# Attention in unbroken runs of turns, scores and values, with the PSUM banks dealt out anew and the scores moved to SBUF by VectorE

## The chip, the cores and the metric

The kernel runs on one core of one Trainium2 chip. The metric is the device time of the whole program in microseconds, as the median of the runs. Everything below is about three stages of a long program; the rest of the program is the same before and after.

## The reference, cut to what matters

The program is two small diffusion-transformer blocks of two layers each, on 512 latent tokens and 256 context tokens of width 1024, all in fp32. Three of its four mixers are attention:

```
def diff_attend(q, k, v, lam):                      # layer 1: 8 heads x 2 maps, 768 keys
    s = jnp.einsum('bqhmd,bkhmd->bhmqk', q, k).astype(jnp.float32) * ATTN_SCALE
    p = jax.nn.softmax(s, axis=-1)
    w = (p[:, :, 0] - lam * p[:, :, 1]).astype(v.dtype)
    return jnp.einsum('bhqk,bkhe->bqhe', w, v)
# layer 2, neighbourhood: 16 heads, a bias on the 512 latent keys, 256 context keys without one
        s_loc = jnp.where(col_in[None, None, :, None, :], s_loc + bias[None].astype(jnp.float32), -jnp.inf)
        s_all = jnp.concatenate([s_loc.reshape(B, NA_HEADS, GRID_W, n_loc), s_ctx], axis=-1)
        prob = jax.nn.softmax(s_all, axis=-1).astype(v_band.dtype)
# layer 3, window: 16 heads, keys at most 128 away and the context, and one sink logit per head
        s_win = jnp.where(ok, s_win, NEG_INF)
        p = sink_softmax(jnp.concatenate([s_win, s_ctx], axis=-1)).astype(vw.dtype)
```

## The kernel before, in words

`attention_stage` is called three times, with `diff=True` (the differential stage), `bias=True` (the bias stage) and `sink=True` (the sink stage). Its work is cut into units. A unit is one pair of heads (or of maps), m = 0 and 1, and one tile of 128 queries; its keys come in blocks of 128, nk of them. There are 8 pairs. In the differential stage a pair has six units in the order 6, 2, 6, 2, 6, 6 key blocks (48 units: I call those with six large, those with two small). In the bias stage a pair has four units of six blocks (32 units). In the sink stage a pair has six units of 4, 2, 5, 2, 5, 4 blocks (48 units).

Each unit goes through these steps, on queues written out by hand. Each engine has its own loop over s, and semaphores tie them:

- TensorE computes scores. The head m uses rows 64m to 64m+63 of the array, so that the two heads of a pair can run side by side. One fp32 matmul is two passes in the trace, and so two records.
- VectorE finds each row's minimum of the (negated) scores (`minima`); in the bias stage it first adds the bias `G`.
- ScalarE makes the exponentials and their sums (`probabilities`).
- VectorE inverts the sums (`inverse_sums`), and in the differential stage combines the two maps into one weight (`combine`).
- TensorE turns the weights, 128 by 128 at a time, four in one PSUM bank (a chunk). It uses the whole array. There are one or two chunks for a unit of the differential stage, three in the bias stage, one to three in the sink stage.
- ScalarE and, for chunk 1 outside the differential stage, VectorE copy the turned blocks to SBUF (`pT_mat`).
- TensorE multiplies them with the values (`weighted`), and VectorE scales the result (`finish`). Outside the differential stage the two heads of `weighted` use different columns of the array.

PSUM has eight banks. Before, the scores of one unit take three banks, columns of m = 0 from the left and of m = 1 from the right, and units take turns on two such sets (banks 0 to 2 and 3 to 5). Banks 6 and 7 (`TB`) take the turned chunks by turns, and bank 7 also the result of `weighted`, and bank 6 the side work on the modulation matrix (`mod_rows`, one per pair, in the differential stage). A score set is free again when ScalarE has read it (`p_done` of the unit two before). Because a set of banks is shared between chunks, results and heads, TensorE's loop deals the work out in pieces:

```
                if s >= 0:
                    turn(s, 0)
                if s + ahead < N:
                    scores_early(s + ahead)
                if s >= 0 and len(chunks[s]) > 1:
                    turn(s, 1)
                if s + ahead < N:
                    scores_late(s + ahead)
                if s >= 0 and len(chunks[s]) > 2:
                    turn(s, 2)
```

and then the modulation and `weighted(s - 1)`. `ahead` is 3 in the differential stage and 2 elsewhere: so far the scores run ahead of the turns.

## Time and profile before

| what | value |
|---|---|
| median of 3 runs | 3873.28 us (3869.57 to 3876.15) |
| span of the profiled execution | 3870.4 us |
| TensorE busy / VectorE busy / ScalarE busy in it | 95% / 57% / 35% |
| differential stage | from 256.0 us, some 208 us |
| bias stage | from 1301.0 us, some 179 us |
| sink stage | from 2035.6 us, some 202 us |
| mean granted TensorE clock | 0.985 |

The times are of the device, of the one core. The span is that of one execution under the profiler, from its first to its last instruction; it stands 2.9 us below the median of the timed runs. PE is TensorE's matmul queue, PEld its weight loads, DVE VectorE, ACT ScalarE, POOL GpSimd. In a timeline each row is a group of like instructions: start in us, duration in us from the first start to the last end, engine, line of the kernel, operation, tiles, how many, and in brackets how long the engine had stood idle and what ended that. `issue` there means that nothing the profile shows released it.

### The profile page before, as it was taken

To read this page: it belongs to the slowest core of one execution; us is meant where nothing else is said; L and a number is where in the kernel's file an instruction comes from. 1 tells how busy PE (TensorE), PEld (TensorE's weight loads), DVE (VectorE), ACT (ScalarE), POOL (GpSimd) and SP (SyncE) were. 2 spreads that over 40 slices of the span, in tenths; PEclk is the share of its full clock that TensorE was granted. 3 is DMA by queue.
4 is the path that set the end of the run, shared out by engine and by line. 5 is a ranking of instruction groups with operands and counts; after the bars stand their busy time and mean duration, and the time that the engine had idled before them with its cause. 6 is when DMAs were issued, how large, how long until landed. Compare 5 with 4: busy or idle time off the path is not lost. (4 is left out here: it accounts for less than half of the span.)

```text
span 3870.4 us, 54090 instructions
## 1 busy us (share of the span) xinstructions
PE 3668.5 (95%) x20171; PEld 2984.9 (77%) x20171; DVE 2209.8 (57%) x3167; ACT 1338.7 (35%) x2342; POOL 833.0 (22%) x588
## 2 busy tenths in 40 slices
PE   7988899999999899999999999999989998899998
PEld 5876688888878677777786678888878876687886
DVE  5746646556573475444436647656665637846445
ACT  3346532121243454222325522212123334523222
POOL 2500012313132111222220011221310007901222
PEclk9999999999999999999999999999999999999999
DMA  5134223322322311544320013233221141032222
GB/s 183 66 120 131 66 77 115 114 100 102 113 67 68 85 45 42 188 152 155 113 65 10 1 44 135 104 113 114 105 74 55 57 142 33 23 109 96 98 93 72
DMA packets 191993, 352.38 MB, mean 91 GB/s; under 512 B 42236, under 2 KB 43853, under 8 KB 191821
## 3 DMA queue, kind: packets, MB, share of 16 engines
q1 hardware_dynamic: 187693, 340.83, 26.4%
q10 hardware_dynamic: 4144, 9.44, 0.7%
q8 instruction: 102, 1.67, 0.2%
q14 instruction: 54, 0.44, 0.0%
HBM read 341.71 MB, written 16.92 MB: 93 GB/s over the span
## 5 line engine op out<-in xcount | busy, mean ns | idle before, releaser
L569 POOL TENSOR_TENSOR x<-x,scaled_buf 128x512 f32<-128x512 f32 (+1 forms) x360 | 495.1, 1391 | 2202.1 <-DVE scaled_buf L561 2201.7
L129 DVE TENSOR_TENSOR w_lo<-raw,w_hi 128x2048 fp32r<-128x2048 f32 x198 | 465.6, 2351 | 685.0 <-ACT w_hi L123 675.7
L123 ACT ACTIVATE w_hi<-raw 128x2048 fp32r<-128x2048 f32 x197 | 377.1, 1914 | 1286.3 <-PE psum L386 1283.9
L384 PE MATMUL psum<-hT_hi,w_hi 128*128 128x512 f32 (+1 forms) x1888 | 669.0, 354 | 2.4 <-DVE hT_lo L848 1.5
L385 PE MATMUL psum<-hT_lo,w_hi 128*128 128x512 f32 (+1 forms) x1888 | 665.1, 352 | 0.0
L386 PE MATMUL psum<-hT_hi,w_lo 128*128 128x512 f32 (+1 forms) x1888 | 664.5, 352 | 0.0
L384 PE MATMUL psum<-w_hi,uT_hi 128*128 128x512 f32 x1280 | 503.0, 393 | 0.0
L386 PE MATMUL psum<-w_hi,uT_lo 128*128 128x512 f32 x1280 | 498.7, 390 | 0.0
L385 PE MATMUL psum<-w_lo,uT_hi 128*128 128x512 f32 x1280 | 498.2, 389 | 0.0
L561 DVE TENSOR_TENSOR scaled_buf<-psum,gate 128x512 f32<-128x512 f32 x360 | 244.8, 688 | 337.3 <-PE psum L386 291.9
L384 PE MATMUL psum<-w_hi,hT_hi 128*128 128x512 f32 x1072 | 419.8, 392 | 2.2 <-issue 1.2
L386 PE MATMUL psum<-w_hi,hT_lo 128*128 128x512 f32 x1072 | 417.6, 390 | 0.0
L385 PE MATMUL psum<-w_lo,hT_hi 128*128 128x512 f32 x1072 | 417.3, 389 | 0.0
L384 PEld LDWEIGHTS psum<-hT_hi,w_hi 128*128 128x128 f32 x1888 | 358.4, 190 | 51.4 <-DVE hT_lo L848 1.9
L385 PEld LDWEIGHTS psum<-hT_lo,w_hi 128*128 128x128 f32 x1888 | 358.4, 190 | 48.0
L386 PEld LDWEIGHTS psum<-hT_hi,w_lo 128*128 128x128 f32 x1888 | 357.8, 190 | 48.7
L384 PEld LDWEIGHTS psum<-w_hi,uT_hi 128*128 128x128 f32 x1280 | 240.4, 188 | 51.1 <-issue 3.5
L386 PEld LDWEIGHTS psum<-w_hi,uT_lo 128*128 128x128 f32 x1280 | 240.3, 188 | 50.8
L385 PEld LDWEIGHTS psum<-w_lo,uT_hi 128*128 128x128 f32 x1280 | 240.6, 188 | 48.0
L384 PEld LDWEIGHTS psum<-w_hi,hT_hi 128*128 128x128 f32 x1072 | 201.6, 188 | 44.8 <-issue 3.6
L386 PEld LDWEIGHTS psum<-w_hi,hT_lo 128*128 128x128 f32 x1072 | 201.4, 188 | 42.1
L385 PEld LDWEIGHTS psum<-w_lo,hT_hi 128*128 128x128 f32 x1072 | 201.6, 188 | 40.9
(286 smaller groups left out, 4918.4 us busy)
## 6 DMA issues: line engine op xcount, KB each, us to landing
raw<-in_w_mlp SPq DMA_DIRECT2D x64, 1024.0 KB, 5.2
raw<-in_ff_w SPq DMA_DIRECT2D x64, 1024.0 KB, 5.3
mod_wide<-in_w_mod SPq DMA_DIRECT2D x32, 1536.0 KB, 8.5
mod_wide<-in_w_mod SPq DMA_DIRECT2D x8, 3072.0 KB, 10.5
raw<-in_ssm_w_in SPq DMA_DIRECT2D x20, 1024.0 KB, 5.1
mod_slab<-in_w_mod SPq DMA_DIRECT2D x8, 2048.0 KB, 8.4
raw<-in_a_w_qkv SPq DMA_DIRECT2D x12, 1024.0 KB, 5.1
raw<-in_b_w_qkv SPq DMA_DIRECT2D x12, 1024.0 KB, 5.1
```

Source lines behind the costliest of these rows:

```text
L123: act.activation(K.w_hi[h][:, :, :], K.raw[h][:, :, :], ACT.Copy).then_inc(K.hi_done.h, 1)
L129: dve.tensor_tensor(K.w_lo[h][:, :, :], K.raw[h][:, :, :], K.w_hi[h][:, :, :].bitcast(F32), ALU.subtract).then_inc(K.lo_done.h, 1)
L384: pe.matmul(out, hi_a, hi_w, start=first, stop=False, **check)
L385: pe.matmul(out, hi_a, lo_w, start=False, stop=False, **check)
L386: return pe.matmul(out, lo_a, hi_w, start=False, stop=last, **check)
L561: dve.tensor_tensor(K.scaled_buf[:, j % 2, :], bank[:, :], K.gate[:, cls, ds(n * SLAB_N, SLAB_N)], ALU.mult)\
L569: pool.tensor_tensor(x, x, K.scaled_buf[:, j % 2, :], ALU.add).then_inc(K.added.h, 1)
```

## The change

What it does:

- The scores of head m have two banks of their own (0 and 1, 2 and 3), and there is one such set instead of two. The turned chunks 0, 1 and 2 have a bank each (4, 5 and 6; 4 and 5 in the differential stage). The result of `weighted` has its own bank (7; 6 in the differential stage, where the modulation has 7).
- TensorE's loop becomes: all turns of unit s, all scores of unit s + ahead, [modulation,] all of `weighted(s - 1)`. `ahead` is 4 and 3. A unit's score matmuls are up to 512 keys wide, and alternate between the heads.
- VectorE no longer only reads the scores to find the minimum: `taken` copies them from PSUM to `p_mat` in SBUF, with the minimum as the second output; in the bias stage the addition of the bias writes there too. ScalarE's exponential then works in place in SBUF.
- The next unit's scores wait for that copy (`s_read`, one count per head) where they waited for ScalarE two units back.
- VectorE's order is changed: inverse (and combine) first, then the copy of chunk 1 (as before, outside the differential stage), minima, finish. ScalarE copies its chunks together.
- `p_mat` has four slots in the differential stage, three elsewhere.

The diff, cut to what the text speaks of:

```
-        self.nk = len(keys[0])
-        self.width = self.nk * P
-        self.at = (0, 12 - self.nk)
-        self.shares = self.nk > 4
+        self.nk = len(keys)
+        self.at = (0, self.nk)
...
+        runs = []
+        for i, kt in enumerate(self.keys):
+            if runs and i % 4 and self.keys[i - 1] == kt - 1 and (kt in self.unrotated) == (kt - 1 in self.unrotated):
+                runs[-1][2] += 1
+            else:
+                runs.append([i, kt, 1])
+        return runs
...
-    ahead = 3 if diff else 2
+    ahead = 4 if diff else 3
+    p_mat, pT_mat = (K.p_mat_diff, K.pT_mat_diff) if diff else (K.p_mat, K.pT_mat)
...
-    scores_of = [K.psum[:, 3 * b:3 * b + 3, :].rearrange("p a b -> p (a b)") for b in range(2)]
-    S = lambda v: scores_of[v % 2]
-    TB = [K.bank[6], K.bank[7]]
-    ap0, sharing = K.apart.n, [sum(u.shares for u in units[:v]) for v in range(N + 1)]
+    S = [K.psum[:, 2 * m:2 * m + 2, :].rearrange("p a b -> p (a b)") for m in range(2)]
+    TB = [K.bank[4 + c] for c in range(2 if diff else 3)]
+    OB, MB = (K.bank[6], K.bank[7]) if diff else (K.bank[7], None)
...
-            def turn(v, c):
-                b = c % 2
-                if c == 0 and diff:
+            def turns(v):
+                if diff:
                     pe.wait_ge(K.w_done.h, at(K.w_done, v))
-                elif c == 0:
+                else:
                     pe.wait_ge(K.p_done.h, at(K.p_done, 2 * v + 1))
-                pe.wait_ge(K.pt_read[b].h, at(K.pt_read[b], order[v, c] - 1))
-                if b == 1:
-
-                    pe.wait_ge(K.o_read.h, at(K.o_read, v - 2))
-                for i, col in enumerate(chunks[v][c]):
-                    mm = pe.transpose(TB[b][:, i * P:(i + 1) * P], K.p_mat[:, v % 3, col * P:(col + 1) * P], K.ident[:, :])
-                mm.then_inc(K.pt_done[b].h, 1)
-
-            def score(v, run, opens):
+                for c, blocks in enumerate(chunks[v]):
+                    pe.wait_ge(K.pt_read[c].h, at(K.pt_read[c], order[v, c] - 1))
+                    for i, col in enumerate(blocks):
+                        mm = pe.transpose(TB[c][:, i * P:(i + 1) * P], p_mat[:, v % ahead, col * P:(col + 1) * P], K.ident[:, :])
+                    mm.then_inc(K.pt_done[c].h, 1)
+
+            def scores(v):
                 u = units[v]
-                _, m, col, kt, n = run
-                rows = slice(m * HEAD_DIM, (m + 1) * HEAD_DIM)
-                return pe.matmul(S(v)[:, col * P:(col + n) * P], q_of(u.pair, u.tile, kt in u.unrotated)[rows, :],
-                                 k_of(u.pair, kt, n, rows), start=opens, stop=True, skip_group_check=True)
-
-            def scores_early(v):
-                u = units[v]
-
-                pe.wait_ge(K.p_done.h, at(K.p_done, 2 * (v - 2) + 1))
-                for run in u.segments()[0]:
-                    mm = score(v, run, True)
-                    if u.shares and run[1] == 1:
-                        mm.then_inc(K.apart.h, 1)
-                if not u.segments()[1]:
-                    mm.then_inc(K.s_done.h, 1)
-
-            def scores_late(v):
-                u = units[v]
-                opened = set(run[2] // 4 for run in u.segments()[0])
-                for m in range(2):
-                    for kt, mask in u.masks.items():
-                        col = u.at[m] + u.keys[m].index(kt)
-                        pe.matmul(S(v)[:, col * P:(col + 1) * P], K.ident_a[:, :], mask, start=col // 4 not in opened, stop=True,
+                opened = set()
+                for kt, mask in u.masks.items():
+                    for m in range(2):
+                        col = u.keys.index(kt)
+                        if not opened or opened == {(0, col // 4)}:
+                            pe.wait_ge(K.s_read.h, at(K.s_read, 2 * (v - 1) + m))
+                        pe.matmul(S[m][:, col * P:(col + 1) * P], K.ident_a[:, :], mask, start=(m, col // 4) not in opened, stop=True,
                                   skip_group_check=True)
-                        opened.add(col // 4)
-                for run in u.segments()[1]:
-                    if u.shares and run[2] // 4 == 1:
-
-                        pe.wait_ge(K.apart.h, ap0 + sharing[v] + 1)
-                    mm = score(v, run, run[2] // 4 not in opened)
-                    opened.add(run[2] // 4)
-                if u.segments()[1]:
-                    mm.then_inc(K.s_done.h, 1)
+                        opened.add((m, col // 4))
+                for col, kt, n in u.segments():
+                    for m in range(2):
+                        rows = slice(m * HEAD_DIM, (m + 1) * HEAD_DIM)
+                        if col == 0 and not u.masks:
+                            pe.wait_ge(K.s_read.h, at(K.s_read, 2 * (v - 1) + m))
+                        mm = pe.matmul(S[m][:, col * P:(col + n) * P], q_of(u.pair, u.tile, kt in u.unrotated)[rows, :],
+                                       k_of(u.pair, kt, n, rows), start=(m, col // 4) not in opened, stop=True, skip_group_check=True)
+                        opened.add((m, col // 4))
+                mm.then_inc(K.s_done.h, 1)
...
                 if s >= 0:
-                    turn(s, 0)
+                    turns(s)
                 if s + ahead < N:
-                    scores_early(s + ahead)
-                if s >= 0 and len(chunks[s]) > 1:
-                    turn(s, 1)
-                if s + ahead < N:
-                    scores_late(s + ahead)
-                if s >= 0 and len(chunks[s]) > 2:
-                    turn(s, 2)
+                    scores(s + ahead)
                 if s in rows_at:
-                    modulation_rows(s)
-                if s in cols_at:
-                    modulation_columns(s)
+                    modulation_rows(rows_at[s])
                 if s >= 1:
                     weighted(s - 1)
+                if s in cols_at:
+                    modulation_columns(cols_at[s])
             weighted(N - 1)
...
-            def copied(v, c):
-                dst, src = turned(act, v, c)
-                act.activation(dst, src, ACT.Copy).then_inc(K.pt_read[c % 2].h, 1)
+            def copied(v):
+                act.wait_ge(K.o_done.h, at(K.o_done, v - 2))
+                for c, blocks in enumerate(chunks[v]):
+                    if c == 1 and not diff:
+                        continue
+                    act.wait_ge(K.pt_done[c].h, at(K.pt_done[c], order[v, c]))
+                    n = len(blocks) * P
+                    act.activation(pT_mat[:, v % 2, c * 4 * P:c * 4 * P + n], TB[c][:, 0:n], ACT.Copy).then_inc(K.pt_read[c].h, 1)
...
                 for m in range(2):
-                    act.activation(K.p_mat[:, v % 3, u.span(m)], S(v)[:, u.span(m)], ACT.Exp, bias=K.neg_max[:, v % 4, m:m + 1],
+                    if diff:
+                        act.wait_ge(K.s_read.h, at(K.s_read, 2 * v + m))
+                    p = p_mat[:, v % ahead, u.span(m)]
+                    act.activation(p, p, ACT.Exp, bias=K.neg_max[:, v % 4, m:m + 1],
                                    scale=-1.0, accum_out=K.p_sum[:, v % 4, m:m + 1]).then_inc(K.p_done.h, 1)
...
+                if v >= ahead:
+                    for c in range(len(chunks[v - ahead])):
+                        dve.wait_ge(K.pt_done[c].h, at(K.pt_done[c], order[v - ahead, c]))
+                nm, p = K.neg_max[:, v % 4, :], p_mat[:, v % ahead, :]
+                taken = lambda m, a, b, low: dve.tensor_scalar(p[:, (u.at[m] + a) * P:(u.at[m] + b) * P], S[m][:, a * P:b * P], 1.0, 3e38,
+                                                               ALU.mult, ALU.min, accum_out=low)
                 if bias:
                     if u.tile == 0:
                         dve.wait_ge(K.g_ready.h, at(K.g_ready, u.pair))
                     row = N_ROWS - 1 - 2 * u.tile
                     for m in range(2):
-                        x = s[:, 0:4 * P] if m == 0 else s[:, 8 * P:12 * P]
                         g = K.G[u.pair % 2][:, m, row:row + N_ROWS, :].rearrange("p r c -> p (r c)")
-                        dve.tensor_tensor_reduce(x, x, g, 1.0, 3e38, ALU.add, ALU.min, nm[:, m:m + 1])
-                    link(dve.tensor_reduce(K.ctx_min[:, v % 4, :], s[:, 4 * P:8 * P].rearrange("p (m c) -> p m c", m=2), AX.X, ALU.min))
+                        dve.tensor_tensor_reduce(p[:, u.at[m] * P:(u.at[m] + LAT_TILES) * P], S[m][:, 0:N_LAT], g, 1.0, 3e38, ALU.add, ALU.min,
+                                                 nm[:, m:m + 1])
+                        taken(m, LAT_TILES, TOK_TILES, K.ctx_min[:, v % 4, m:m + 1]).then_inc(K.s_read.h, 1)
+                    dve.wait_ge(K.s_read.h, at(K.s_read, 2 * v + 1))
                     dve.tensor_tensor(nm, nm, K.ctx_min[:, v % 4, :], ALU.min).then_inc(K.nm_done.h, 1)
                     return
-                if u.nk == 6:
-                    ins = dve.tensor_reduce(nm, s.rearrange("p (m c) -> p m c", m=2), AX.X, ALU.min)
-                else:
-                    for m in range(2):
-                        ins = dve.tensor_reduce(nm[:, m:m + 1], s[:, u.span(m)], AX.X, ALU.min)
...
             for s in range(-ahead, N):
-                if diff and 0 <= s + 1 < N:
-                    combine(s + 1)
+                if 0 <= s + ahead - 2 < N:
+                    inverse_sums(s + ahead - 2)
+                    if diff:
+                        combine(s + ahead - 2)
                 if not diff and s >= 0 and len(chunks[s]) > 1:
-                    dst, src = turned(dve, s, 1)
-                    dve.tensor_copy(dst, src).then_inc(K.pt_read[1].h, 1)
+                    copied(s, 1)
...```

How the change moves TensorE's instructions in the steady part of the bias stage. A row is one line's matmuls in program order; `p_mat` is turned, `qkv` gives queries and keys, `pT_mat` is multiplied with the values, `p_inv` spreads the inverse sums. Before, one unit:

```order
L1722 MATMUL psum<-ident,p_mat 128x128 x4
L1729 MATMUL psum<-qkv 128x256 x2
L1722 MATMUL psum<-ident,p_mat 128x128 x4
L1729 MATMUL psum<-qkv 128x256
L1729 MATMUL psum<-qkv 128x512
L1729 MATMUL psum<-qkv 128x256
L1722 MATMUL psum<-ident,p_mat 128x128 x4
L1778 MATMUL psum<-pT_mat,qkv 64x128 x12
L1783 MATMUL psum<-ident,p_inv 64x128 x2
```

And after the change, one unit:

```order
L1703 MATMUL psum<-ident,p_mat 128x128 x12
L1722 MATMUL psum<-qkv 128x512 x2
L1722 MATMUL psum<-qkv 128x256 x2
L1740 MATMUL psum<-pT_mat,qkv 64x128 x12
L1745 MATMUL psum<-ident,p_inv 64x128 x2
```

Three groups of turns and two of scores have become one group each; the number of turned blocks and of key columns is the same.

VectorE in the same place of the bias stage, one unit before the change. L1887 is the addition of the bias with its minimum (and, in the row after it, the read-out of the minimum):

```order
L1939 COPY pT_mat<-psum 128x512
L1887 ISA psum,neg_max<-psum,G_128 128x512
L1887 ISA neg_max 128x1
L1887 ISA psum,neg_max<-psum,G_128 128x512
L1887 ISA neg_max 128x1
L1888 TENSOR_REDUCE ctx_min<-psum 128x2
L1889 TENSOR_TENSOR neg_max<-neg_max,ctx_min 128x2
L1909 RECIPROCAL p_inv<-p_sum 128x2
L1928 COPY inv_rows<-psum 128x128
L1929 TENSOR_TENSOR qkv<-psum,inv_rows 128x128
```

And after it:

```order
L1873 COPY pT_mat<-psum 128x512
L1838 ISA p_mat,neg_max<-psum,G_130 128x512
L1838 ISA neg_max 128x1
L1830 TENSOR_SCALAR p_mat,ctx_min<-psum 128x256
L1838 ISA p_mat,neg_max<-psum,G_130 128x512
L1838 ISA neg_max 128x1
L1830 TENSOR_SCALAR p_mat,ctx_min<-psum 128x256
L1842 TENSOR_TENSOR neg_max<-neg_max,ctx_min 128x2
L1881 COPY inv_rows<-psum 128x128
L1882 TENSOR_TENSOR qkv<-psum,inv_rows 128x128
L1859 RECIPROCAL p_inv<-p_sum 128x2
```

One reduction over both heads' context columns has become two copies with a minimum, and the reciprocal has moved behind the finish.

VectorE in the differential stage, one large unit's minimum among its neighbours, before (L1892 is the minimum of both maps in one instruction):

```order
L1892 TENSOR_REDUCE neg_max<-psum 128x2
L1909 RECIPROCAL p_inv<-p_sum 128x2
L1913 TENSOR_SCALAR p_inv<-p_sum,p_inv,neg_lam 128x1
L1926 TENSOR_SCALAR qkv<-psum,p_inv 128x128
L1919 SCALAR_TENSOR_TENSOR p_mat<-p_mat,p_inv 128x256
```

And after:

```order
L1830 TENSOR_SCALAR p_mat_diff,neg_max<-psum 128x768 x2
L1879 TENSOR_SCALAR qkv<-psum,p_inv 128x128
L1859 RECIPROCAL p_inv<-p_sum 128x2
L1865 TENSOR_SCALAR p_inv<-p_sum,p_inv,neg_lam 128x1
L1867 SCALAR_TENSOR_TENSOR p_mat_diff<-p_mat_diff,p_inv 128x256
```

One instruction over 1536 columns has become two over 768, and inverse and combination of a unit now stand together, after the finish.

## Rows read from the trace of the kernel before

**Rows 1.** The stages: window, its us, busy PE, PEld, DVE, ACT, POOL, PEclk, DMA.

```profile
256.00:464.00 208.00, 174.60 (x1216) 120.85 (x1216) 139.58 (x272) 128.59 (x378) 0.00 (x0) 0.98 0.42 122
1301.00:1480.30 179.30, 168.51 (x1600) 122.91 (x1600) 117.98 (x320) 96.27 (x193) 27.24 (x6) 0.97 0.15 36
2035.60:2237.60 202.00, 183.54 (x1728) 131.44 (x1728) 130.37 (x417) 101.36 (x305) 0.00 (x0) 0.97 0.01 1
```

**Rows 2.** Timeline, bias stage, one unit's step in the steady part.

```profile
1400.95 0.42 PEld L1722 LDWEIGHTS psum<-ident,p_mat 128*128 128x128 f32 x4 [0.17 <-issue]
1401.54 0.30 PEld L1729 LDWEIGHTS psum<-qkv 64*128 64x128 f32 x4 [0.17 <-issue]
1402.17 0.42 PEld L1722 LDWEIGHTS psum<-ident,p_mat 128*128 128x128 f32 x4 [0.33 <-issue]
1402.75 0.73 PEld L1729 LDWEIGHTS psum<-qkv 64*128 64x128 f32 x6 [0.17 <-issue]
1403.81 0.42 PEld L1722 LDWEIGHTS psum<-ident,p_mat 128*128 128x128 f32 x4 [0.33 <-issue]
1403.94 0.70 DVE L1887 CUSTOM_DVE_ANT_0 psum<-psum,G 128x512 f32<-128x512 f32 x1 [0.38 <-PE psum L1729]
1404.40 1.29 PEld L1778 LDWEIGHTS psum<-pT_mat,qkv 128*64 128x64 f32 x24 [0.17 <-issue]
1404.55 0.73 DVE L1887 CUSTOM_DVE_ANT_0 psum<-psum,G 128x512 f32<-128x512 f32 x1
1405.20 0.69 DVE L1888 TENSOR_REDUCE ctx_min<-psum 128x2 f32<-128x512 f32 x1
1406.08 0.42 PEld L1722 LDWEIGHTS psum<-ident,p_mat 128*128 128x128 f32 x4 [0.17 <-issue]
```

**Rows 3.** Timeline, bias stage, behind its last scores: eight turns in a row.

```profile
1469.72 1.12 PE L1722 MATMUL psum<-ident,p_mat 128*128 128x128 f32 x8 [0.22 <-DVE qkv L1929]
```

**Rows 4.** Timeline, sink stage: one row a pair apart, and a small unit's values.

```profile
2080.29 0.16 DVE L1899 TENSOR_TENSOR neg_max<-neg_max,sink_neg 128x2 f32<-128x2 f32 x1
...
2104.26 0.16 DVE L1899 TENSOR_TENSOR neg_max<-neg_max,sink_neg 128x2 f32<-128x2 f32 x1
...
2110.41 0.42 PEld L1778 LDWEIGHTS psum<-pT_mat,qkv 128*64 128x64 f32 x8 [0.17 <-issue]
...
2111.21 0.42 PEld L1722 LDWEIGHTS psum<-ident,p_mat 128*128 128x128 f32 x4 [0.17 <-issue]
```

**Rows 5.** Timeline, differential stage: modulation rows a pair apart, and values.

```profile
394.94 1.90 PE L942 MATMUL psum<-mod_slab,cT 128*2 128x512 f32 x16
396.77 1.60 PE L1776 MATMUL psum<-qkv,pT_mat 128*128 128x128 f32 x12
...
420.04 1.90 PE L942 MATMUL psum<-mod_slab,cT 128*2 128x512 f32 x16
```

**Rows 6.** Groups of instructions by line and shape, VectorE: busy us, mean ns.

```profile
L1892 DVE TENSOR_REDUCE neg_max<-psum 128x2 f32<-128x1536 f32 x32 | 56.2, 1755 | 22.0 <-PE psum L1729 21.8
L1895 DVE TENSOR_REDUCE neg_max<-psum 128x1 f32<-128x256 f32 x64 | 24.0, 416 | 0.5
L1634 DVE TENSOR_SCALAR qkv<-psum 128x512 f32<-128x512 f32 x28 | 18.1, 686 | 34.1 <-PE psum L1616 34.1
L1887 DVE DVE_READ_ACCUMULATOR2_ANT neg_max<- 128x1 f32 x64 | 9.1, 142 | 0.0
L1919 DVE SCALAR_TENSOR_TENSOR p_mat<-p_mat,p_inv 128x768 f32<-128x768 f32 x32 | 32.3, 1010 | 0.1
L1939 DVE COPY pT_mat<-psum 128x512 f32<-128x512 f32 x64 | 44.3, 692 | 70.0 <-PE psum L1722 70.0
```

**Rows 7.** Groups of instructions by line and shape, ScalarE: from PSUM, from SBUF.

```profile
L1827 ACT ACTIVATE pT_mat<-psum 128x256 f32<-128x256 f32 x64 | 24.6, 384 | 30.4 <-PE psum L1722 30.4
L1827 ACT ACTIVATE pT_mat<-psum 128x512 f32<-128x512 f32 x144 | 86.0, 597 | 194.5 <-PE psum L1722 194.5
L1981 ACT ACTIVATE hT_hi<-qkv 128x1024 fp32r<-128x1024 f32 x10 | 9.7, 1046 | 10.7 <-PEq L1685 10.7
```

More of the change, by code:

```diff
@@ L1521, in segments @@
     def segments(self):
[L1525 to L1537 removed]
+        runs = []
[5 more added lines that the diff above has]
+        return runs
     def chunks(self, heads):
[L1541 removed]
+        blocks = range(heads * self.nk)
         return [blocks[c:c + 4] for c in range(0, len(blocks), 4)]
@@ L1829, in probabilities @@
             def probabilities(v):
                 u = units[v]
-                act.wait_ge(K.nm_done.h, at(K.nm_done, v))
-                if v >= 3:
-                    for b in range(2):
-                        if last_turn(v - 3, b) is not None:
-                            act.wait_ge(K.pt_done[b].h, at(K.pt_done[b], last_turn(v - 3, b)))
+                if bias or sink:
+                    act.wait_ge(K.nm_done.h, at(K.nm_done, v))
                 if sink:
@@ L3210, in program @@
         mixed = [0, 4, 1, 5, 2, 3]
-        attention_stage(K, [Unit(p, t, (every if t < LAT_TILES else [4, 5],) * 2) for p in range(PAIRS) for t in mixed], q_of, k_of,
+        attention_stage(K, [Unit(p, t, every if t < LAT_TILES else [4, 5]) for p in range(PAIRS) for t in mixed], q_of, k_of,
                         lambda pair, m, kt: K.qkv[:, kt, 2 * D + pair * P:2 * D + (pair + 1) * P],
```

161 lines of the change are left out of this document (68 added, 93 removed).

## The prediction, made before the changed kernel was run

> **What bounds the kernel now.** I read the clock and the share of each engine first, then the three attention stages as windows [rows 1], then the waits and the timeline inside each. Only these stages change. TensorE is busy for 175 of 208 us, 169 of 179 and 184 of 202; VectorE for 140, 118 and 130; DMA is idle or nearly so in two of them. So TensorE sets the pace, and what is to be read is how its time is spent. The bias stage shows it best, since it repeats exactly [rows 2]: a step takes 1406.08 - 1400.95 = 5.13 us, and consists of turns 0.59, early scores 0.63, turns 0.58, late scores 1.06, turns 0.59, values 1.68. Nothing outside TensorE is waited for. But each time that its use of the array changes (whole for turns, rows in halves for scores, columns in halves for values) the weight loads stand idle for 0.17 us, and 0.33 us behind scores, released by nothing. The early group has 256 columns for each head, the late one 512, and the difference is 0.43 us: so a score group costs 0.20 us plus 0.43 for each two key blocks of both heads. A pass over 128 columns costs 0.11 us when it stands in a run (12 passes to the next load: (1.60 - 0.27)/12, [rows 5]; eight turns last 1.12 with the tail of 0.27, [rows 3]).
>
> The other two stages repeat by pairs: 2104.26 - 2080.29 = 23.97 us in the sink stage [rows 4], 420.04 - 394.94 = 25.10 us in the differential stage [rows 5]. Of the latter TensorE is busy 84%: there it also waits for the engines around it.
>
> **The change, part by part.**
>
> Bias stage, TensorE. Twelve turns in a run: 0.59 + 8 x 0.11 = 1.47. One score group: 0.63 + 2 x 0.43 = 1.49. Values as before, 1.68. The step becomes 4.64 us, 0.49 less. No column is saved; what goes is two turn groups' and one score group's change of array use. 30 full steps give 15 us.
>
> Is TensorE then still the bound? VectorE is busy 118.0/32 = 3.69 us per unit [rows 1]. It loses the context minimum (0.69, [rows 2]) and gains two copies of 256 columns with a minimum. The trace shows no such operation. Its floor is the plain reduction of as many columns, 0.416, without a read-out; my price adds the read-out of 0.142 [rows 6]. That the copy itself is not dearer is seen at 512 columns, where a tensor_scalar from PSUM takes 0.686, as long as the minimum over the context. So + 2 x 0.56 - 0.69 = + 0.43, and 4.1 us of 4.64: TensorE remains the bound.
>
> The new wait: the scores of unit v + 1 wait for VectorE's copy of unit v, since there is one score set. Behind that wait stand the next values and turns on TensorE. Scores that start at 0 are seen by VectorE at 1.49 + 0.13 (1403.94 is 1.19 behind 1402.75, for a group of 1.06). It then takes 0.65 + 0.42 for each head and 0.14 for the last read-out: released at 3.9 us. TensorE wants them at 4.64. The wait is covered, by values and turns, with 0.7 us to spare; without that cover each 0.1 us costs 3 us in the stage.
>
> Sink stage, per pair (22 key blocks in six units). TensorE: 44 turns x 0.11 and 0.15 for each of six groups, 5.7; scores 22 x 0.215 + 6 x 0.20 = 5.9; twelve masks at 0.11, 1.3; values: the two-block unit takes 2111.21 - 2110.41 = 0.80 [rows 4], six blocks 1.68 [rows 2], so 0.22 a block and 0.36 a unit, 7.0. Sum 19.9. VectorE: 130.4/8 = 16.3 [rows 1], and twelve read-outs, 18.0. The units differ in size, and a step of TensorE joins the turns of one, the scores of another and the values of a third: taking step by step whichever engine is later I get 20.3, and allow 0.4 for late releases: 20.7 against 23.97, 8 x 3.3 = 26 us.
>
> Differential stage, per pair. TensorE: 28 turns 3.7, scores 4 x 1.49 + 2 x 0.63 = 7.2, values 56 passes x 0.11 = 6.2, modulation 1.83 (396.77 - 394.94) and its turns 0.4, changes of use 0.5: 19.8. VectorE: 139.6/8 = 17.5 [rows 1]. Two copies of 768 columns cost 2 x (0.95 + 0.14) = 2.2 for one reduction of 1.755: the 0.95 is the line through 256 and 512 columns, (0.686 - 0.416)/256 = 1.05 ns a column [rows 6]. Four times + 0.43 and twice + 0.28: 19.7. The two sums are equal, but not the steps. In the order of the six steps TensorE needs 3.2, 5.5, 1.5, 4.1, 1.9, 3.7 from one unit's scores to the next (the 5.5: modulation rows 1.83, values 1.33, turns 0.86, scores 1.49), VectorE 3.1, 3.7, 3.7, 3.0, 3.1, 2.6 (minima, finish, inverse, and 1.01 us of combination for a large unit, [rows 6]). With one score set neither can be more than a fraction of a unit ahead, about 1.5 us behind the release for a large one. Walked through, the steps are 3.5, 5.5, 3.7, 3.1, 3.1, 3.3: 22.2 against 25.1, 8 x 2.8 = 22 us after rounding down. So here the modulation rows, squeezed between scores and values, keep a part of the gain.
>
> ScalarE. Its exponentials now read SBUF. From PSUM 256 columns take 384 ns and 512 take 597, by which 1024 would take 1023; from SBUF they take 1046 [rows 7]. So 23 ns for each of 256 exponentials, 6 us of an engine that is busy for 129 of 208 us where it is fullest, and idle for TensorE's turns: nothing. The Trainium skill, VectorE: DVE Perf Modes, section on the TRN2 errata, gives ScalarE 224 cycles of fixed cost from SBUF and 172 from PSUM, an estimate of 43 ns each and 11 us in all. The trace shows about half of that; the sum would be the same by either.
>
> Ends of the stages. One more unit is scored before the first turn, each one behind VectorE's copy: some 2 to 3 us more per stage. At the other end the last steps have no scores: in the bias stage two such units now take 1480.3 - 1469.7 = 10.6 us; afterwards three follow at 1.47 + 1.68 = 3.15 each. I take these as even. The lower bound has them as a gain of 6 us in the bias stage.
>
> Sum: 15 + 26 + 22 = 63 us. 3870.4 - 63 = 3807 for the profiled execution, whose span lies 2.9 us below the median: **3810 us**.
>
> **The rivals.**
>
> 1. The forecast: TensorE's rhythm shortens in all stages and few waits replace what went. 3788 to 3832. For it: rows 2, where every idle stretch of the loads is a change of use. 0.55.
>
> 2. Better still: no release is late. Differential 19.9 (- 42), sink 19.9 (- 32), bias with its end (- 21): 3778. Against it stand the unequal steps. 0.08.
>
> 3. The single score set becomes the bound: VectorE's copy comes later than counted (semaphores, a copy that waits for the turns), 0.3 us in each of 128 units. 63 - 38 = 25 us: 3848. For it: in the differential stage both engines are at 19.7 of 22. 0.22.
>
> 4. Given back in full, or a stage held by something else (the modulation's loads): 3873. Against it: DMA works 42% of the stage's time. 0.05.
>
> 5. Slower: the copy with a minimum runs at a lower rate than the reduction. If it takes twice as long, VectorE needs 19.7 + 9.3 = 29.0 a pair in the differential stage (+ 31 us), 23.9 in the sink stage (none), 5.0 in the bias stage (- 5): 3899. It decides from about 1.8 times the price, 1.7 us for 768 columns. For it: a combination of two inputs takes 1010 ns for 768 columns, and the operation is new here. Against it: the bias addition with its minimum costs 0.61 to 0.65 per 512 columns [rows 2], hardly more than a reduction. 0.10.
>
> **How the numbers follow.** A measurement of this kernel can tell about 0.2%, 7.7 us, from no change. Rivals 1 to 3 are faster: 0.85; same 0.05; slower 0.10. The range holds the first case, most of the third and a part of the second: 3785 to 3858; the likeliest case's own is 3788 to 3832.
>
> **What would show it.** Bias stage: a step of 4.6 us, with one idle 0.33 us and two of 0.17 before loads. Sink: 20 to 21.5 us a pair. Differential: 22 to 23.5, TensorE waiting for VectorE after small units and VectorE for TensorE after the modulation rows. The copy of 768 columns at 0.95 us. Wrong would be: a copy over 1.3 us, scores that wait for `s_read` in every step, turns that wait for the combination, or a bias step over 4.9.

## The result

The changed kernel takes 3803.09 us (3802.08 to 3803.63, four runs) against 3874.55 us before (3869.57 to 3876.15, four runs). The ratio is 0.9815, with a 95% interval of 0.9801 to 0.9829: 71.5 us or 1.85% faster. 3810 was predicted, with 3785 to 3858. The profiled execution has a span of 3800.3 us against 3870.4, 70.1 us less.

The three stages, as windows from the first scores to the last `finish` (us, busy PE, PEld, DVE, ACT, POOL, then the granted clock, DMA share and GB/s), to be held against [rows 1]:

```profile
255.90:441.30 185.40, 176.74 (x1152) 118.81 (x1152) 146.96 (x400) 127.76 (x376) 0.00 (x0) 0.99 0.48 137
1279.60:1442.50 162.90, 155.07 (x1536) 114.99 (x1536) 120.47 (x416) 98.87 (x193) 27.30 (x6) 0.97 0.17 40
1998.30:2167.00 168.70, 164.73 (x1728) 134.08 (x1728) 128.95 (x513) 104.75 (x305) 0.00 (x0) 0.98 0.01 2
```

| stage | before | after | less | predicted |
|---|---|---|---|---|
| differential | 207.6 | 185.4 | 22.2 | 22 |
| bias | 179.2 | 162.8 | 16.4 | 15 |
| sink | 201.6 | 168.7 | 32.9 | 26 |

The columns before and after are the first scores' start to the last `finish`, from the two traces. They add up to 71.5, against 70.1 between the spans of the same two traces: the three stages hold the whole gain. Ahead of, between and behind them no stretch changed by more than 1.0 us, and together these are 1.4 us longer. TensorE is busy for 95% of the differential stage, where it was busy for 84% before; its work hardly changed (174.6 to 176.7 us), but its pauses went.

The steady step of the bias stage, in the timeline (start, us, engine, line, operation, tiles, and in brackets the idle time before it and what ended it); it answers to [rows 2]:

```profile
1358.26 1.29 PEld L1703 LDWEIGHTS psum<-ident,p_mat 128*128 128x128 f32 x12 [0.17 <-issue]
1359.72 0.30 PEld L1722 LDWEIGHTS psum<-qkv 64*128 64x128 f32 x4 [0.17 <-issue]
...
1361.21 1.29 PEld L1740 LDWEIGHTS psum<-pT_mat,qkv 128*64 128x64 f32 x24 [0.33 <-issue]
1361.33 0.69 DVE L1838 CUSTOM_DVE_ANT_0 p_mat<-psum,G 128x512 f32<-128x512 f32 x1 [1.25 <-PE psum L1722]
...
1362.89 1.19 PEld L1703 LDWEIGHTS psum<-ident,p_mat 128*128 128x128 f32 x11 [0.17 <-issue]
1363.25 0.08 DVE L1830 DVE_READ_ACCUMULATOR p_mat<-psum 128x1 f32 x1
```

Twelve turns take 1.46, the one score group 1.49, the values 1.68: 4.63 us, where the prediction had 1.47, 1.49, 1.68 and 4.64. Of the six idle stretches that a step had for a change of array use, three are left: 0.17, 0.17 and 0.33. VectorE has read the second head 3.61 us after the scores started (1363.33 - 1359.72; predicted 3.9), 1 us before TensorE wants the bank (1364.35).

The sink stage repeats after exactly 20.0 us, where [rows 4] had 23.97, and the differential stage after 22.09, where [rows 5] had 25.10:

```profile
2042.70 0.16 DVE L1849 TENSOR_TENSOR neg_max<-neg_max,sink_neg 128x2 f32<-128x2 f32 x1
...
2062.70 0.16 DVE L1849 TENSOR_TENSOR neg_max<-neg_max,sink_neg 128x2 f32<-128x2 f32 x1
```

```profile
338.79 1.90 PE L942 MATMUL psum<-mod_slab,cT 128*2 128x512 f32 x16
...
360.88 1.90 PE L942 MATMUL psum<-mod_slab,cT 128*2 128x512 f32 x16
```

The new operations, in the groups by line and shape (busy us, mean ns, idle before them), beside [rows 6, 7]:

```profile
L1830 DVE TENSOR_SCALAR_CACHE_REDUCE p_mat_diff<-psum 128x768 f32<-128x768 f32 x64 | 58.8, 955 | 11.2 <-PE psum L1722 11.2
L1830 DVE TENSOR_SCALAR_CACHE_REDUCE p_mat<-psum 128x256 f32<-128x256 f32 x96 | 39.1, 419 | 1.8 <-PE psum L1722 1.8
L1830 DVE DVE_READ_ACCUMULATOR p_mat<-psum 128x1 f32 x160 | 13.2, 83 | 0.0
L1792 ACT ACTIVATE p_mat<-p_mat,neg_max 128x768 f32<-128x768 f32 x64 | 59.0, 925 | 11.2 <-DVE neg_max L1842 11.2
```

The copy with a minimum costs what the bare minimum of as many columns costs (0.955 us for 768 columns, as the bare minimum in experiment 4; 0.419 for 256, where the bare minimum had 0.416), and its read-out takes 83 ns. The prediction had priced it by the 142 ns of the bias addition's read-out in the kernel before. The exponential of 768 columns takes 925 ns from SBUF against 898 from PSUM.

In the waits of the differential stage (us in total, times, longest, from 280 to 410 us) rival 3 can be seen, in small:

```profile
PEld psum L1738 <- issue: 14.8, 35, 0.9
...
DVE qkv L1879 <- PE psum L1738: 10.8, 12, 1.5
PEld psum L1722 <- DVE p_mat_diff L1830: 9.3, 23, 0.6
...
DVE p_mat_diff L1830 <- PE psum L1722: 5.5, 23, 0.3
```

The score loads wait for VectorE's copy 23 times, for 9.3 us in six pairs (some of them hold the 0.17 us that a change of use costs anyway), and VectorE waits for TensorE elsewhere: each in turn, as the prediction's walk through the steps had it.

The prediction did not look at the clock at the start of a stage. In the last 10 us ahead of the changed kernel's bias stage TensorE is busy for 1.8 us, and the granted clock is 0.81; in the first 15 us of the stage it is 0.67, as in the kernel before. In three of the experiments it is 0.50 there, which is the lower of the two levels (1.2 and 2.4 GHz) all the time; why it differs from one execution to another is open. Stages with the same code differ by some 2 us along with it (experiment 5), so a difference of that size can't be put down to an edit without a look at the pairs.

### The profile page after: what moved, and what is told of

The parts are those of the page before. It is cut to its first block and busy times, and to the rows that moved or that the text cites. A ratio compares the mean times of both kernels' runs of the same rounds, so it can differ in the third digit from the quotient of the medians.

```text
span 3800.3 us, 53965 instructions
## 1 busy us (share of the span) xinstructions
PE 3639.9 (96%) x20043; PEld 2979.6 (78%) x20043; DVE 2219.4 (58%) x3487; ACT 1344.4 (35%) x2342; POOL 831.7 (22%) x588
```

## The experiments

Each was timed beside the kernel before, on the same chip; the ratios are to that kernel. "Changed kernel" is the one whose result stands above. It was not timed again beside the experiments, where the kernel before took 3875.3 to 3878.0 us, so differences to 3803 us are good to some 4 us. Pair and step lengths are repeats of the same instruction in the trace.

**1. Pieces again** (`e1_split`). The banks, the copies and VectorE's order stay as in the changed kernel, but TensorE deals its work out in pieces again. The first two key blocks of each head's scores also get a matmul of their own again (not shown), which makes two more score matmuls in a unit of six key blocks; the late score group still takes the 1.06 us that it took before.

```diff
                 if s >= 0:
-                    turns(s)
+                    turns(s, 0)
                 if s + ahead < N:
-                    scores(s + ahead)
+                    scores(s + ahead, False)
+                if s >= 0:
+                    turns(s, 1)
+                if s + ahead < N:
+                    scores(s + ahead, True)
+                if s >= 0:
+                    turns(s, 2)
```

> The changed kernel, with TensorE's loop dealt out in pieces again: turns of chunk 0, scores of the first two key blocks, turns of chunk 1, the other scores, turns of chunk 2. Banks, the copy by VectorE, and how far the scores run ahead stay as changed. Theory 1 (the gain is the changes of array use that went): the bias step returns from 4.63 to 5.13 us, the sink pair from 20.0 to about 22, the differential pair from 22.2 to about 23: 15 + 16 + 6 = 37 us more than the changed kernel's 3803, so 3840. Theory 2 (the gain is in waits: private banks, scores further ahead): less than 10 us more, 3803 to 3813.

Measured: 3850.09 us (3848.07 to 3857.53), ratio 0.9937 (0.9918 to 0.9955). That is 47 us above the changed kernel. The differential pair is 23.34 us long, the sink pair 21.97, the bias step about 5.2. So two thirds of the gain hang on the runs themselves, with all else in place, which is theory 1. By stage, from first scores to last `finish`, the pieces give back 17.1 us in the bias stage, which is all that it had gained, 19.6 of 32.9 in the sink stage and 11.3 of 22.2 in the differential stage. The rest in these two came with the other parts of the change (a bank for each chunk, the copy, VectorE's new order, scores further ahead), and no run divides it among them.

The time is 10 us above theory 1. Eight times the change of a pair gives 39 of the 48 us by which the three stages are longer in the traces; the rest lies mostly at their starts. From the bias stage's first scores to its first `finish` it is 28.3 us here and 21.5 in the changed kernel. The first 15 us of that stage, here and in the changed kernel:

```profile
1291.30:1306.30 15.00, 12.59 (x42) 7.94 (x42) 6.35 (x27) 5.77 (x10) 0.00 (x0) 0.50 0.00 0
...
1279.60:1294.60 15.00, 12.67 (x42) 6.74 (x44) 7.22 (x30) 6.79 (x12) 0.00 (x0) 0.67 0.00 0
```

The clock was granted at 0.50 here and at 0.67 there. How much of the 6.8 us is the clock and how much the pieces was not measured.

**2. No copy** (`e2_nocopy`). VectorE only reduces, and ScalarE's exponential reads the scores from PSUM, so that the one score set is free only when ScalarE is done.

```diff
-pe.wait_ge(K.s_read.h, at(K.s_read, 2 * (v - 1) + m))
+pe.wait_ge(K.p_done.h, at(K.p_done, 2 * (v - 1) + m))
...
-                    act.activation(p, p, ACT.Exp, bias=K.neg_max[:, v % 4, m:m + 1],
+                    act.activation(p, S[m][:, 0:u.nk * P], ACT.Exp, bias=K.neg_max[:, v % 4, m:m + 1],
```

> The changed kernel without the move of the scores to SBUF: VectorE only finds the minimum (and adds the bias in PSUM), ScalarE reads the scores from PSUM, and the next scores wait for ScalarE's exponentials of the unit before, as they must with one score set. Theory 1 (the copy is what makes one score set enough): a bias step becomes turns 1.5, ScalarE's copies and exponentials to 4.5, scores to 6.0, values 1.7: 7.7 us for 4.63, + 89 us; differential about 33 a pair, + 90; sink + 70; together about 4050 (3990 to 4110). Theory 2 (the copy is no necessity, ScalarE lets go of the scores early enough): at most + 30, 3833.

Measured: 4161.16 us (4149.98 to 4169.16), ratio 1.0741 (1.0719 to 1.0763). The waits of this kernel from 340 to 420 us, and the window:

```profile
PEld psum L1722 <- ACT p_mat_diff L1792: 26.0, 24, 2.2
PE psum L1722 <- ACT p_mat_diff L1792: 19.3, 16, 2.0
```

```profile
340.00:420.00 80.00, 61.92 (x300) 39.60 (x299) 37.62 (x77) 30.86 (x96) 0.00 (x0) 0.83 0.27 79
```

The scores now wait for ScalarE, and a differential pair takes 37 to 41 us. Runs of turns with one score set are worth nothing without the copy; the copy that frees the set is the part that everything else leans on. Theory 1 is right in kind, but the time lies outside its range, 110 us above its number. The clock has a part in that: in this stretch TensorE is busy 77% of the time and the granted clock is 0.83, where the changed kernel has 98% and 1.00 in the same stretch. So the work between the waits ran slower too. How the 110 us divide between waits and clock was not measured.

**3. One unit less ahead** (`e3_shallow`), with the buffers as many as before.

```diff
-    ahead = 4 if diff else 3
+    ahead, slots = (3, 4) if diff else (2, 3)
```

> The changed kernel with the scores one unit less ahead of the turns (3 in the differential stage, 2 in the others), all slots kept. Theory 1 (depth only covers; what pays is runs): bias stage the same, since the exponentials end some 2.9 us behind the turns before and the next turns come 3.2 us behind them; differential the same; sink about + 3 us a pair, since there scores and values together can last less than the exponentials; 3 x 2.5 us less at the starts: about 3818 (3800 to 3835). Theory 2 (depth is what pays): + 50 us or more, 3853 and up.

Measured: 3803.14 us (3802.22 to 3806.67), ratio 0.9810 (0.9794 to 0.9826): the same as the changed kernel. But that is a sum of two signs. The differential pair falls from 22.09 to 21.52 us and the stage is 4.9 us shorter; the sink pair rises from 20.00 to 20.95 and the stage is 7.8 us longer. The depth pays in the sink stage and costs in the differential one; why it costs there was not tried. The prediction gave the depth neither a gain nor a loss but the ends of the stages.

**4. VectorE reads everything twice** (`e4_twice`). A second minimum of the same columns, whose result nobody uses, stands ahead of each copy.

```diff
+                        dve.tensor_reduce(K.sink_exp[:, v % 4, m:m + 1], S[m][:, LAT_TILES * P:TOK_TILES * P], AX.X, ALU.min)
...
+                    dve.tensor_reduce(K.ctx_min[:, v % 4, m:m + 1], S[m][:, 0:u.nk * P], AX.X, ALU.min)
```

> The changed kernel, and ahead of each copy of scores VectorE reads the same columns once more for a minimum that nobody uses (in the bias stage the context columns alone). That is what the copy would cost at twice its price (rival 5 of the prediction). By the prediction's arithmetic: VectorE becomes the bound in the differential stage (about 27.8 us a pair for 22.2, + 45) and in the sink stage (about 24 for 20.0, + 31), and nothing happens in the bias stage (0.7 us for each unit within a slack of about 1 us): 3803 + 76 = 3879. If VectorE's work were covered everywhere, as its busy share of 58% suggests: less than + 10.

Measured: 3922.37 us (3922.28 to 3923.61), ratio 1.0120 (1.0103 to 1.0136). The extra work on a large unit, and the differential stage from 340 to 420 us, its waits and its window:

```profile
L1846 DVE TENSOR_REDUCE ctx_min<-psum 128x1 f32<-128x768 f32 x64 | 61.1, 955 | 16.6 <-PE psum L1722 16.3
```

```profile
PEld psum L1722 <- DVE p_mat_diff L1830: 18.5, 16, 1.4
PE psum L1722 <- DVE p_mat_diff L1830: 12.1, 16, 1.1
```

```profile
340.00:420.00 80.00, 67.88 (x371) 43.65 (x371) 68.66 (x155) 40.90 (x120) 0.00 (x0) 0.87 0.38 112
```

The differential pair takes 29 to 33 us, the sink pair 24.42, the bias step 4.92. So VectorE's time between scores and release is what decides between gain and loss. Against the changed kernel 119 us were lost, not 76: 72 in the differential stage where 45 were expected, 41 in the sink stage for 31, and 8 in the bias stage for nothing. In the differential stage neither engine is full (TensorE 85%, VectorE 86%), and TensorE's loads and matmuls stand for VectorE's copy, 18.5 and 12.1 us in 16 times each. The granted clock, 0.87, is lower here too.

**5. A minimum of one input** (`e5_one_input`), in the bias stage.

```diff
-                    dve.tensor_tensor(nm, nm, K.ctx_min[:, v % 4, :], ALU.min).then_inc(K.nm_done.h, 1)
+                    dve.tensor_reduce(nm, K.ctx_min[:, v % 4, :, :], AX.X, ALU.min).then_inc(K.nm_done.h, 1)
```

The reason for it is a row of the changed kernel's trace. This instruction on two columns, 0.16 us as a rule, takes 2.2 to 3.3 us once per pair:

```profile
1360.98 4.55 POOL L1548 TENSOR_TENSOR G<-G,col_mask 128x2048 f32<-128x2048 f32 x1 [14.35 <-DMA G<-skewed_rest]
...
1363.37 2.19 DVE L1842 TENSOR_TENSOR neg_max<-neg_max,ctx_min 128x2 f32<-128x2 f32 x1
...
1366.23 0.99 PE L1740 MATMUL psum<-pT_mat,qkv 128*64 128x128 f32 x14 [0.32 <-DVE qkv L1882]
```

It ends 0.01 to 0.03 us after GpSimd's instruction, six times of six, and then `finish` and TensorE are late.

> The changed kernel, but in the bias stage the two minima of a head are written side by side and their minimum is a reduction of one input (128x4 to 128x2) and no longer a tensor_tensor of two inputs in SBUF. Nothing else changes. Theory 1: the tensor_tensor of two columns, which takes 160 ns as a rule and 2.2 to 3.3 us once in each pair in which GpSimd masks the next bias, is held by GpSimd's instruction, since both have two inputs in SBUF. Then no small operation of VectorE lasts over 0.3 us in the bias stage, its pairs take 18.5 us each (4 x 4.63) in place of 18.8 to 19.7, and the time falls by 3 to 5 us: 3799 (3796 to 3801). Theory 2: VectorE is held by GpSimd whatever the form of the instruction, or by the data of the bias: the reduction takes 2 to 3 us in its place, and the time stays at 3803 (3801 to 3806).

Measured: 3801.78 us (3797.52 to 3802.87), ratio 0.9806 (0.9793 to 0.9820). In the trace the stall is gone, in every pair:

```profile
L1842 DVE TENSOR_REDUCE neg_max<-ctx_min 128x2 f32<-128x4 f32 x32 | 5.0, 157 | 1.1
```

The pairs of the bias stage take 18.52 us each, where the changed kernel has 18.9 to 19.7, and the stage is 2.5 us shorter. So theory 1 holds for the mechanism. The time of the whole kernel misses its range (3796 to 3801), and 1.3 us can't be told from nothing. The trace says what hides the 2.5 us: the differential stage, whose code is the same and whose pairs take the same 22.09 us, is 2.1 us longer, all of it ahead of the first `finish`. The first 15 us of the differential stage, here and in the changed kernel:

```profile
255.50:270.50 15.00, 12.15 (x38) 6.27 (x38) 8.81 (x25) 8.10 (x19) 0.00 (x0) 0.68 0.74 211
...
255.90:270.90 15.00, 11.29 (x42) 5.51 (x42) 10.50 (x30) 9.21 (x21) 0.00 (x0) 0.89 0.72 211
```

The granted clock was 0.68 here and 0.89 there, and 38 matmul passes were done instead of 42.

**6. Modulation moved** (`e6_moved`), in the differential stage.

```diff
-    rows_at = {v: units[v].pair for v in range(N) if mod and units[v].tile == LAT_TILES}
-    cols_at = {v: units[v].pair for v in range(N) if mod and units[v].tile == LAT_TILES + 1}
+    rows_at = {v: units[v].pair for v in range(N) if mod and units[v].tile == 1}
+    cols_at = {v: units[v].pair for v in range(N) if mod and units[v].tile == 2}
```

> The changed kernel, but in the differential stage TensorE's modulation rows are issued in the second step of a pair and the modulation columns in the third, where it scores small units, and no longer in the fifth and sixth. Theory 1 (the prediction's walk through the steps): the 5.5 us step of the rows splits into two even ones, and what stays is the later of both engines' sums: a pair of 20.5 to 21.6 us in place of 22.15, 4 to 13 us in all, 3797 (3790 to 3800). Theory 2: the pair is held by VectorE's copies and the single score set in every step, so the place of 1.83 us of TensorE makes no difference: 3803 (3800 to 3806).

Measured: 3792.44 us (3788.62 to 3793.60), ratio 0.9780 (0.9767 to 0.9794), 10.6 us below the changed kernel. One pair later in the trace:

```profile
335.83 1.90 PE L942 MATMUL psum<-mod_slab,cT 128*2 128x512 f32 x16
356.34 1.90 PE L942 MATMUL psum<-mod_slab,cT 128*2 128x512 f32 x16
```

20.51 us a pair in place of 22.09. The prediction's long step was real: the rows of 1.83 us, squeezed between large scores and large values, kept VectorE waiting. In the changed kernel it stands still for 1.52 us a pair for the values behind the rows:

```profile
342.26 0.35 DVE L1879 TENSOR_SCALAR qkv<-psum,p_inv 128x128 f32<-128x128 f32 x1 [1.52 <-PE psum L1738]
```

With the rows moved, the longest such wait is 0.6 us.

**7. All copies on ScalarE** (`e7_scalar_copies`), in the bias and the sink stage.

```diff
-                    if c == 1 and not diff:
-                        continue
...
-                if not diff and s >= 0 and len(chunks[s]) > 1:
-                    copied(s, 1)
```

> The changed kernel, but ScalarE copies the second group of turned probabilities too in the bias and the sink stage, and VectorE none. Theory 1 (TensorE's own sums set the pace there, both engines have slack): ScalarE goes from 64 to about 78% busy, VectorE from 80 to 65%, and the time stays within 3 us of the changed kernel's: 3803 (3800 to 3808). Theory 2 (VectorE's release of the single score set is what the step waits for): the release comes up to 0.69 us earlier where the copy stood before it, and the time falls by 5 us or more, to 3798 or less. Theory 3: ScalarE, which must copy three groups and make two exponentials in a row, becomes late with the probabilities: turns wait for it, 0.2 us or more a step in 80 steps, 3819 or more.

Measured: 3803.32 us (3800.86 to 3805.88), ratio 0.9812 (0.9799 to 0.9826). The sink pair stays at 20.00 us. That VectorE copies the second group makes no difference: both engines have room for it, and TensorE's own sum sets the pace of these two stages. That is theory 1.

**8. Turns in two groups** (`e9_two_turn_groups`).

```diff
                 if s >= 0:
-                    turns(s)
+                    turns(s, False)
                 if s + ahead < N:
                     scores(s + ahead)
+                if s >= 0:
+                    turns(s, True)
```

> The changed kernel, but a unit's turns are issued in two groups, the first (four key blocks) ahead of the scores and the rest behind them; scores and values stay as they are. So each unit of more than four blocks of turns has one more group of turns and one more change of TensorE's array use, and nothing else. Theory 1 (a change of array use costs TensorE its idle of the weight loads, 0.15 us a turn group, whatever the other engines do): the bias step goes from 4.63 to 4.78 us, the sink pair from 20.0 to about 20.6 (four of six units have more than one group), the differential pair by as much or less, since it is not at TensorE's own sum; together 32 x 0.15 + 32 x 0.15 + up to 32 x 0.15, so 10 to 14 us: 3813 to 3817. Theory 2 (the gain came from the turns being early, so that copies of VectorE and ScalarE have more time, and not from the number of groups): the late turns make copies late by more than a turn group, and the time rises by over 25 us, to 3828 or more. Theory 3 (groups cost nothing by themselves): 3803.

Measured: 3827.27 us (3824.87 to 3828.17), ratio 0.9877 (0.9859 to 0.9895): 24 us, where theory 1 had 10 to 14 and theory 2 over 25. Neither number is met. The sink pair is at 21.27, the differential at 23.03, the bias pair at 19.51. The timeline of the bias stage says why:

```profile
1360.58 1.33 PEld L1724 LDWEIGHTS psum<-qkv 64*128 64x128 f32 x8 [0.17 <-issue]
...
1362.24 0.85 PEld L1705 LDWEIGHTS psum<-ident,p_mat 128*128 128x128 f32 x8 [0.33 <-issue]
1362.94 0.69 DVE L1877 COPY pT_mat<-psum 128x512 f32<-128x512 f32 x1 [1.44 <-PE psum L1705]
...
1365.45 0.08 DVE L1834 DVE_READ_ACCUMULATOR p_mat<-psum 128x1 f32 x1
1365.54 0.35 PEld L1724 LDWEIGHTS psum<-qkv 64*128 64x128 f32 x4 [0.17 <-DVE p_mat L1834]
```

VectorE stands idle for 1.44 us until the late group of turns comes, and only then turns to its minima. It ends them at 1365.53, just when TensorE wants the bank. So the second group costs twice: its own change of use, and a late release.

**9. The same, with all copies on ScalarE** (`e10_two_groups_scalar`), which takes that copy out of VectorE's way: the edits of 7 and 8 together.

> As the kernel with two turn groups, but ScalarE copies the second group of turned probabilities in the bias and the sink stage, so that VectorE no longer waits there for the turns behind the scores (1.44 us idle in a bias step of the run before) ahead of its minima. Theory 1: of the 0.32 us that a second turn group cost, 0.15 is TensorE's change of use and the rest is the second head's scores, released 0.17 us late by VectorE. Then the bias step becomes 4.78 us, the sink pair 20.6, the differential pair stays at 23.03, where ScalarE made the copies already: 162 + 5, 168 + 5, 192 us, and the time 3827 - 5 - 5 = 3817 (3814 to 3820). Theory 2: a second turn group costs 0.32 on TensorE by itself: bias step 4.95, sink pair 21.3, 3827. Theory 3: the late copy makes ScalarE late in its place (two copies and two exponentials behind the turns): 3827 or more.

Measured: 3820.22 us (3817.31 to 3820.53), ratio 0.9856 (0.9839 to 0.9872). The sink pair falls from 21.27 to 20.71, 0.71 above the changed kernel's for four units with a second group: 0.18 a group, near the 0.15 of theory 1. The bias stage kept most of its loss (steps up to 4.90, where theory 1 had 4.78), and so the time is just above theory 1's range of 3814 to 3820. There the wait only moved:

```profile
DVE p_mat L1840 <- PE psum L1705: 37.4, 22, 2.4
```

From 1320 to 1430 us VectorE's minima wait for the turns themselves, because they write into the `p_mat` slot that the late group still reads. So a price near 0.15 is shown in the sink stage alone.

**10. Three edits together** (`e8_together`): 5, 6, and in the differential stage three units ahead (four slots kept), with three ahead elsewhere.

```diff
-    ahead = 4 if diff else 3
+    ahead, slots = (3, 4) if diff else (3, 3)
```

> The changed kernel with three edits: the minimum of one input in the bias stage, the modulation rows and columns in the second and third step of a pair, and in the differential stage scores three units ahead and no longer four (the stage in which the shallower kernel was 4.9 us shorter between its first scores and its last values; the sink stage, where it was 7.9 us longer, keeps three units ahead). If the three gains add: 4 + 6 + 5 = 15 us, 3788 (3782 to 3794). If moving the rows and the shallower depth give the same slack back, 4 + 6 = 10 us: 3793. If only the first holds: 3799.

Measured: 3781.69 us (3778.15 to 3783.53), ratio 0.9754 (0.9740 to 0.9767), the fastest of all: 21.4 us below the changed kernel, where the three gains as expected added up to 15; it lies just below the expected 3782 to 3794. In the trace the differential stage is 17.2 us shorter than the changed kernel's and the bias stage 5.1. Half of the latter is the edit (2.5 in experiment 5); the other half lies ahead of the first `finish`, where the granted clock in the first 15 us was 0.78 here and 0.50 in experiment 5. The pairs take 19.97, 18.52 and 20.00 us, and from 280 to 410 us TensorE's row shows no idle time:

```profile
280.00:410.00 130.00, 130.00 (x938) 88.72 (x936) 115.96 (x330) 102.11 (x310) 0.00 (x0) 1.00 0.57 164
```

## Why the prediction was right

- **What bounds the kernel** (TensorE's rhythm, with the changes of array use as what is to be had): right, and shown by experiments 1 and 7, and by 9 for the sink stage. The Trainium skill, TensorEngine Tiling (Array Packing), Key Properties, says that changing the tiling mode drains TensorE. The rows agree: the weight loads idle for 0.17 us at each change of use, and 0.33 behind scores.
- **Bias stage, - 15**: - 16.4. The step was met to 0.01 us. The prediction called the stage exactly periodic. It isn't: once per pair GpSimd holds VectorE (experiment 5). By the pairs' lengths this costs 0.6 us a pair in the changed kernel (19.1 on average for 18.52) and some 0.7 in the one before (21.3 for 4 x 5.13, where no run took the hold away), so it hardly changes the difference.
- **Sink stage, - 26**: - 32.9. This is the term that was mis-sized: a pair was put at 20.7 and takes 20.0, 5.6 us in eight pairs. TensorE's own sum was put at 19.9, close to that; the 20.3 of the uneven steps and the 0.4 for late releases were not there. The walk let each step be ruled by its later engine; but with three units ahead, VectorE's long steps seem to be made up for in the short ones. Experiment 3 speaks for that: with two ahead the pair takes 20.95.
- **Differential stage, - 22**: - 22.2. The pair was forecast at 22.2 and takes 22.09. Here luck had a part. The walk had steps of 3.5, 5.5, 3.7, 3.1, 3.1 and 3.3 us; from one unit's scores to the next the trace has 3.24, 5.77, 2.63, 4.12, 2.79 and 3.54. The walk had one step at 3.1 where its own sum for TensorE was 4.1, and the errors of up to 1.1 us cancel from step to step. VectorE's six steps also add up to 19.2 and not to the 19.7 named beside them. The cause given for what is left, the modulation rows, was right (experiment 6), and TensorE's own sum of 19.8 can nearly be reached (19.97, experiment 10).
- **The copy's price**: 0.955 us for 768 columns as interpolated. The read-out was taken at 142 ns and is 83, and in the timeline the next addition starts with the read-out, 0.34 us behind the copy's start and not 0.42: so the release comes at 3.6 and not at 3.9 us.
- **ScalarE at nothing**: right; experiment 7 gave ScalarE more copies to do in two stages, and the time stayed. The exponential of 768 columns costs 27 to 34 ns more from SBUF, where 23 were counted.
- **Rival 3** (the single set binds) is true of a part of the differential stage only, 9.3 us of waits in 130. **Rival 5** had the right mechanism, but too low a price. It gave 3899 for a copy of twice the price, and experiment 4, with as much added, measured 3922. It had the differential stage 31 us longer than before, and 50 were measured; no loss in the sink stage, where 8 were measured (24.42 a pair for 23.97); and no lower clock. As an estimate, a straight line between 3803 and 3922 crosses the 3875 of the kernel before at 1.6 times the price and not at 1.8.
- **The ends of the stages** were taken as even, and the clock at their starts was not looked at. In the differential stage the first `finish` comes 20.1 us after the first scores where it came after 15.8, and the last pair takes 15.4 us where it took 19.2, so there the two are nearly even.

## What to carry to other kernels

Where an engine pauses at each change between kinds of work, count the groups per unit and not only the work: here twelve turns in one group in place of three, and one score group in place of two, gave some 47 of 71 us without one column less. A single buffer can stand in for two if an engine empties it at once; then the time between "full" and "free" is the number to watch, and everything that stands ahead of the emptying in that engine's order belongs to it. And put side work in the step where its engine has least to do: moving 1.83 us of it was worth 1.6 us a pair. Last, judge a small edit by its steady steps: the granted clock at the start of a stage moved whole times here by as much as the edit did.

## What was not expected of the hardware

A VectorE instruction on two columns with both inputs in SBUF waits until GpSimd's running instruction of 4.55 us ends (2.2 to 3.3 us instead of 0.16 in the changed kernel, 1.2 to 1.8 in the one before, six of six in each). The same minimum as a reduction of one input takes 0.157 us at the same place, and VectorE's copies from PSUM and its bias addition with one input in PSUM run at their usual 0.69 us beside GpSimd. The Trainium skill, SBUF — State Buffer, section on the two separate sides, states just this: the two engines share a pair of ports, a VectorE instruction with two SBUF inputs needs it against a GpSimd instruction that reads SBUF, and whoever starts first holds it for its whole instruction. The durations given here agree.

The two heads' score passes run beside each other in two halves of the array. In experiment 8, where the second head's bank came late, its passes started 0.18 us behind the first head's (1360.762 against 1360.585) and stayed behind to the end of the group: the score group took 1.66 us and not 1.49. Every second score group of that bias stage took 1.62 to 1.66 us, the others 1.54. So half a release that is late can cost the whole group.
